# Four-layer transformer kernel: router in column groups, picks ahead of the extra turns, token parts by halves, modulation chunks of layer 0 moved

## Chip, cores, metric

One core of one Trainium2 chip. The time is the device time of one execution in microseconds. The kernel before takes 2621.84 us, the median of three runs (2620.9 to 2629.41).

## What is computed

x has 256 tokens of 1024 values, in float32. Two blocks of two layers each are applied. In the kernel's count, layers 0 and 1 are the first block (attention and a gated feed-forward part with a short convolution), layers 2 and 3 the second (a state-space and a gated linear-attention mixer, then a feed-forward part). Each layer is modulated by a vector that is computed from c by a 1024 x 6144 product. Layer 3's feed-forward part is a mixture of eight experts; the change is mostly about it:

```python
def _moe_swiglu(x, w_router, b_router, w_gate, w_up, w_down):
    logits = (x @ w_router).astype(jnp.float32) + b_router.astype(jnp.float32)
    top_vals, top_idx = lax.top_k(logits, TOP_K)            # TOP_K = 2
    top_w = jax.nn.softmax(top_vals, axis=-1)
    combine = jnp.sum(jax.nn.one_hot(top_idx, N_EXPERTS, dtype=jnp.float32) * top_w[..., None], axis=-2)
    out = jnp.zeros_like(x)
    for e in range(N_EXPERTS):                              # N_EXPERTS = 8, width 3584
        out = out + combine[..., e:e + 1].astype(x.dtype) * _swiglu(x, w_gate[e], w_up[e], w_down[e])
    return out
```

## The kernel before

It is written by hand for five engines, each with its own instruction list; semaphores order them, and every wait stands in the code. Weights come in chunks of 1 MB through a ring of seven slots; SyncE issues the loads in the order of chunk_plan, each as soon as TensorE has used the chunk seven places before. ScalarE (ACT) writes a chunk's leading part in fp32r, VectorE (DVE) or GpSimd (POOL) the rest in place, and TensorE (PE) sums three products of such parts (lines 847 to 849), which gives float32 exactness at the fp32r rate.

**Layer 0, projections (PE lines 1226 on, DVE line 2765).** Fifteen column chunks in the order PROJ_ORDER. The first three (i = 0, 1, 2) are multiplied whole in float32 (L675), the others by parts. The parts of hT are written by ACT early and by DVE (L2769), on DVE behind the low part (L2106) of the fourth chunk. After each projection one of layer 0's modulation chunks 8 to 23 is multiplied (ada_sum, L577: eight products of 256 columns in four column groups of the array), two after the last.

**Normalization of layers 2 and 3 (post_layer, DVE L2246 to L2264).** For each half t of the tokens: gate, residual, statistics, a power on POOL (L1393), centring (L2264, "normed"). PE transposes x (L615), ACT and DVE evict the blocks of hT with scale and shift (blocks b = 0, 2 by ACT, 1, 3 by DVE), and POOL meanwhile applies gain and shift to x itself (gains, L1417 and L1419, four operations on 128x1024).

**Router (PE L1259, L1261; DVE route, L2701).** For each half of the tokens eight products of hT's 128 columns (as weights) with the router's 8 columns, then the bias. DVE copies the logits (L2705), takes the maximum, the differences (L2709, which ACT exponentiates), ranks every logit against the others, and marks the two best ("chosen").

**Places, picks, extra turns (DVE mixture, L2306).** An expert has room for 128 tokens; an expert chosen by more gets an extra turn, up to three. PE counts places with five small products (L1182 to L1185); DVE makes the places (L2315 on; "placed"), then the list of turns with the extra ones (L2327 to L2346; "turns"), then the selection matrices pick and pick_w of the first turn (picks, L2350, L2351). xn, in which the output is summed, is set to zero at L2311. PE gathers the first expert's tokens (pick_tiles, L1118), ACT writes them with scale and shift as xg in eight pieces and then its leading part xg_hi whole, DVE the low part whole (x_part, L2361).

**Expert turns (body).** A turn has 42 chunks: for g = 0 to 6 two of gate and two of up, then, one group later, two of down. The first turn ("first") is written out, the others are a loop over turns. PE waits for moe_lo (DVE, L2371) or, for every second down chunk, moe_lo_pool (POOL, L1361). Near the end of a turn (j = 37) PE gathers the next expert's tokens. At the turn's last step ACT writes xg and xg_hi and then the leading part of the transposed products; DVE writes their low part (L2386) and xg's. In the profile w_gate is loaded 126 times, 14 for each of nine turns.

## Time and profile before

| | us |
|---|---|
| median of three runs | 2621.84 |
| the profiled execution | 2623.3 |
| its span, first to last instruction | 2621.5 |
| mean granted TensorE clock | 0.974 of full |
| PE busy | 2487.1 (95%) |
| DVE busy | 1792.8 (68%) |
| ACT busy | 1320.4 (50%) |
| POOL busy | 675.3 (26%) |
| HBM read | 691.10 MB, 264 GB/s over the span |

A row of a timeline gives start, duration, engine, line, operation, output and inputs, the count of merged instructions, and in brackets the idle time in front of it with what ended it. A float32 product shows as two instructions. "ring" and "region" are the weight slots and the working space, with the ending _part when they are written as fp32r. L1468 is the helper of all ACT operations.

### The profile page before, as it was taken

What the parts mean: (1) busy time and instruction counts of PE and PEld (TensorE: products, weight loads), DVE (VectorE), ACT (ScalarE), POOL (GpSimd) and SP (SyncE); (2) the same over time, 40 slices, a digit from 0 to 9 for tenths busy, and PEclk for the clock granted to TensorE, in tenths of its full rate; (3) what the DMA queues carried; (4) which work ended last, traced back from release to release, by engine and by line L of the source; (5) the groups of instructions that cost most, each with busy time, mean ns of one, the idle gap of its engine ahead of it and who ended that gap; (6) DMA issues with size and microseconds to landing.
All of it is one profiled execution on the core that took longest, in us unless ns stands there. A gap on an engine that the chain in (4) does not pass through costs nothing. (4 is left out here: it accounts for less than half of the span.)

```text
span 2621.5 us, 37532 instructions
## 1 busy us (share of the span) xinstructions
PE 2487.1 (95%) x14758; PEld 2043.2 (78%) x14758; DVE 1792.8 (68%) x2022; ACT 1320.4 (50%) x1368; POOL 675.3 (26%) x355
## 2 busy tenths in 40 slices
PE   6999999998999998999887999999999999999996
PEld 4875998985998767899674787878787888888884
DVE  1664776574866947755874777777778777777785
ACT  1434543444443133333131676767676766677773
POOL 0000000003900808700631132323232332323223
PEclk9999999999999998999997999999999999999998
DMA  9996864476874756955332899999999999999992
GB/s 338 288 322 219 260 204 149 154 258 218 263 217 147 237 197 218 288 185 167 107 113 66 303 347 349 348 351 346 346 350 345 344 351 338 357 334 361 327 366 109
DMA packets 434956, 693.86 MB, mean 265 GB/s; under 512 B 37690, under 2 KB 255894, under 8 KB 434838
## 3 DMA queue, kind: packets, MB, share of 16 engines
q1 hardware_dynamic: 407632, 677.17, 75.2%
q10 hardware_dynamic: 27206, 15.03, 2.1%
q8 instruction: 85, 1.39, 0.2%
q14 instruction: 33, 0.27, 0.0%
HBM read 691.10 MB, written 1.05 MB: 264 GB/s over the span
## 5 line engine op out<-in xcount | busy, mean ns | idle before, releaser
L1468 ACT ACTIVATE region_part<-ring 128x2048 fp32r<-128x2048 f32 x448 | 835.6, 1907 | 274.0 <-PE bank L849 194.6
L849 PE MATMUL bank<-ring_part,region_part 128*128 128x512 f32 x1648 | 648.7, 394 | 0.0
L2371 DVE TENSOR_TENSOR ring_part<-ring,region_part 128x2048 fp32r<-128x2048 f32 x270 | 640.4, 2405 | 1.7 <-ACT region_part L1468 1.7
L847 PE MATMUL bank<-region_part 128*128 128x512 f32 x1432 | 582.3, 407 | 6.2 <-DVE ring_part L2371 6.2
L848 PE MATMUL bank<-region_part 128*128 128x512 f32 x1296 | 511.7, 395 | 0.0
L1361 POOL TENSOR_TENSOR ring_part<-ring,region_part 128x2048 fp32r<-128x2048 f32 x54 | 268.2, 4974 | 554.8 <-ACT region_part L1468 554.8
L849 PEld LDWEIGHTS bank<-ring_part,region_part 128*128 128x128 f32 x1648 | 309.7, 188 | 71.3
L847 PE MATMUL bank<-xn_part,region_part 128*128 128x256 f32 x1152 | 327.3, 284 | 10.0 <-DVE hT_part L2074 9.1
L847 PEld LDWEIGHTS bank<-region_part 128*128 128x128 f32 x1432 | 269.4, 188 | 75.5 <-issue 14.6
L849 PE MATMUL bank<-hT_part,region_part 128*128 128x256 f32 x1152 | 325.6, 283 | 0.0
L848 PE MATMUL bank<-xn_part,ring_part 128*128 128x256 f32 x1152 | 325.4, 282 | 0.0
L2029 DVE TENSOR_TENSOR ring_part<-ring,region_part 128x2048 fp32r<-128x2048 f32 x72 | 175.4, 2444 | 177.5 <-ACT region_part L1468 177.5
L1393 POOL TENSOR_TENSOR stat<-stat,minus_half 128x1 f32<-128x1 f32 (+1 forms) x36 | 21.7, 602 | 1058.0 <-DVE stat L2005 580.7
L848 PEld LDWEIGHTS bank<-region_part 128*128 128x128 f32 x1296 | 243.6, 188 | 60.1 <-issue 7.7
L1468 ACT ACTIVATE region<-bank 128x512 f32<-128x512 f32 (+1 forms) x172 | 94.5, 573 | 366.2 <-PE bank L849 241.1
L847 PEld LDWEIGHTS bank<-xn_part,region_part 128*128 128x128 f32 x1152 | 219.3, 190 | 14.7 <-DVE hT_part L2074 10.7
L848 PEld LDWEIGHTS bank<-xn_part,ring_part 128*128 128x128 f32 x1152 | 220.1, 191 | 1.4
L849 PEld LDWEIGHTS bank<-hT_part,region_part 128*128 128x128 f32 x1152 | 219.4, 190 | 0.0
L2382 DVE TENSOR_TENSOR region<-bank,region 128x512 f32<-128x512 f32 x63 | 43.5, 691 | 167.7 <-issue 166.8
L1361 POOL TENSOR_TENSOR ring_part<-ring,hT_part 128x2048 fp32r<-128x2048 f32 x9 | 55.5, 6172 | 286.6 <-ACT hT_part L1468 286.6
L1468 ACT ACTIVATE region_part<-bank 128x512 fp32r<-128x512 f32 x63 | 37.6, 597 | 165.2 <-PE bank L1161 165.2
L577 PE MATMUL bank<-ring,c_wide 128*32 128x256 f32 x1536 | 105.0, 401 | 9.3 <-DMA ring<-in_w_ada 9.3
(321 smaller groups left out, 3990.4 us busy)
## 6 DMA issues: line engine op xcount, KB each, us to landing
ring<-in_moe_w_gate SPq DMA_DIRECT2D x126, 1024.0 KB, 5.1
ring<-in_moe_w_up SPq DMA_DIRECT2D x126, 1024.0 KB, 5.2
ring<-in_moe_w_down SPq DMA_DIRECT2D x126, 1024.0 KB, 5.0
ring<-in_w_ada SPq DMA_DIRECT2D x48, 1024.0 KB, 7.4
ring<-in_mod_w SPq DMA_DIRECT2D x48, 1024.0 KB, 6.7
ring<-in_w_in SPq DMA_DIRECT2D x44, 1024.0 KB, 5.7
ring<-in_w_up_act SPq DMA_DIRECT2D x22, 1024.0 KB, 5.5
ring<-in_w_up_lin SPq DMA_DIRECT2D x22, 1024.0 KB, 5.8
```

The costliest lines, as they stand in the source:

```text
L577: m = nc.tensor.matmul(o[r:r + 32, 0:CW], c_wide[:, k, AT - q:AT - q + 32], w[:, k, :], start=q == first and k < 4, stop=k >= 4, skip_grou ...
L847: nc.tensor.matmul(o, split(a_hi), split(b_hi), start=start, stop=False, skip_group_check=True)
L848: nc.tensor.matmul(o, split(a_lo), split(b_hi), start=False, stop=False, skip_group_check=True)
L849: return nc.tensor.matmul(o, split(a_hi), split(b_lo), start=False, stop=stop, skip_group_check=True)
L1361: nc.gpsimd.tensor_tensor(split(w), w, whole(hi), ALU.subtract).then_inc(*done("moe_lo_pool", j, e))
L1393: nc.gpsimd.tensor_tensor(dst, dst, minus_half[:, 0:dst.shape[1]], ALU.pow).then_inc(*done("rstd", *key))
L1468: return nc.scalar.activation(out_, in_, func, **kw).then_inc(*done(*event))
L2029: v.tensor_tensor(split(chunk(key)), chunk(key), whole(hi_part(key)), ALU.subtract).then_inc(*done("w_lo", *key))
L2371: v.tensor_tensor(split(w), w, whole(hi), ALU.subtract).then_inc(*done("moe_lo", j, e))
L2382: v.tensor_tensor(moe_h, psum[2 * (g % 2) + 1], moe_s, ALU.mult).then_inc(*done("moe_h", g, e))
```

## The change

Layer 0's modulation chunks: none after the first three projections, then one or two after each. The router multiplies hT (256 columns) by 8-column weights in four column groups, two blocks k in each, as the blocks become ready; the bias is added third; ACT and DVE copy the four groups' partial sums into router_out (the place of spread, set to zero before), two more products turn them, and DVE's reduction adds the four groups. POOL's gains wait for both halves of the normalization. xn is set to zero by POOL behind the gains. The extra turns are computed behind the first turn's picks, low parts and token parts, with the first three low parts brought forward. Both picks come before both pick_w, and the gather waits only for the picks. xg_hi and xg's low part are made in two halves, and TensorE waits for the second half only at the second chunk.

```diff
@@ -62,6 +62,8 @@
 IN_WHOLE = 3
+ADA_FIRST = {3: (8,), 4: (9,), 5: (10,), 6: (11,), 7: (12,), 8: (13,), 9: (14, 15), 10: (16,), 11: (17, 18), 12: (19,), 13: (20, 21),
+             14: (22, 23)}
 IDX_PAIRS = [((0, 0), (0, 1)), ((1, 0), (1, 1)), ((1, 2), (1, 3))]
@@ -235,7 +237,7 @@
                 if l == 0:
-                    for q in ([8 + i] if i < 14 else [22, 23]):
+                    for q in ADA_FIRST.get(i, ()):
                         plan.append((("ada", 0, q), ("pe_used", "ada", 0, q)))
@@ -430,6 +432,7 @@
     moe_hi = [cm("", n=SLOT) for _ in range(SLOTS - 1)] + [hT.rearrange("p k s -> p (k s)")]
+    router_out = spread
     turns = nc.alloc_sbuf_tensor("turns", [P, TURNS], mybir.dt.int32)[:, :]
@@ -1102,6 +1105,33 @@
+            def route():
+                halves = [bank(("router", h), ("logits", h), (5 + h,)) for h in range(2)]
+                logits = bank(("logits",), ("logits", 2), (7,))
+                pe.wait_ge(*until("router_loaded"))
+                pe.wait_ge(*until("router_b_loaded"))
+                for b in range(4):
+                    pe.wait_ge(*until("hTd" if b % 2 else "hT", 3, "ffn", b))
+                    for i in range(2):
+                        k = 2 * b + i
+                        g = k % 4
+                        m = nc.tensor.matmul(halves[g // 2][32 * g:32 * g + NE, 0:S], router[:, k, :], hT[:, k, :],
+                                             start=k < 4, stop=k >= 4, skip_group_check=True)
+                    if b == 1:
+                        for t in range(NT):
+                            nc.tensor.matmul(halves[0][0:NE, t * P:(t + 1) * P], router_b[0:1, :], ones[0:1, :],
+                                             start=False, stop=False, skip_group_check=True)
+                    if b >= 2:
+                        m.then_inc(*done("pe_tile", "router", b - 2))
+                pe.wait_ge(*until("router_out", 1))
+                pe.wait_ge(*until("logits", 1))
+                pieces = ident.rearrange("p (g c) -> p g c", g=4)[:, :, 0:NE]
+                for t in range(NT):
+                    m = nc.tensor.matmul(logits[:, t * 4 * NE:(t + 1) * 4 * NE].rearrange("p (g c) -> p g c", g=4),
+                                         router_out[:, t * P:(t + 1) * P], pieces, start=True, stop=True)
+                m.then_inc(*done("pe_tile", "logits"))
             def mixture():
@@ -1110,7 +1140,7 @@
                         pe.wait_ge(*until("x_gained", 3, "mix", 1))
-                    pe.wait_ge(*(until("moe_pick", e) if r is None else within(r, 0, "moe_pick", e)))
+                    pe.wait_ge(*(until("moe_pick_one", 1, e) if r is None else within(r, 0, "moe_pick_one", 1, e)))
                     for b in range(2):
@@ -1128,8 +1158,8 @@
                     for j, (what, g, a) in enumerate(TURN):
-                        if j == 0:
-                            pe.wait_ge(*(until("moe_xg_lo", "start") if r is None else within(r, 1, "moe_xg_lo", e)))
+                        if j < 2:
+                            pe.wait_ge(*(until("moe_xg_lo", j, "start") if r is None else within(r, 1, "moe_xg_lo", j, e)))
                         if what == "gate" and a == 0:
@@ -1229,7 +1259,7 @@
                         if l == 0:
-                            for q in ([8 + i] if i < 14 else [22, 23]):
+                            for q in ADA_FIRST.get(i, ()):
                                 ada_sum(0, 1, q, 8)
@@ -1250,17 +1280,7 @@
                 if l == 3:
-                    hT_ready(l, "ffn")
-                    pe.wait_ge(*until("router_loaded"))
-                    pe.wait_ge(*until("router_b_loaded"))
-                    o = bank(("router",), ("logits",))
-                    for t in range(NT):
-                        for k in range(KD):
-                            nc.tensor.matmul(o[:, t * NE:(t + 1) * NE], hT[:, k, t * P:(t + 1) * P], router[:, k, :],
-                                             start=k == 0, stop=False)
-                        m = nc.tensor.matmul(o[:, t * NE:(t + 1) * NE], ones[0:1, :], router_b[0:1, :],
-                                             start=False, stop=True)
-                    m.then_inc(*done("pe_tile", "router"))
+                    route()
                     mixture()
@@ -1412,6 +1432,7 @@
                 pool.wait_ge(*until(f"rows_{stage}{l}", 1))
+                pool.wait_ge(*until("normed", l, stage, 1))
                 for t in range(NT):
@@ -1452,6 +1473,7 @@
                     gains(l, "mix")
+                    nc.gpsimd.memset(xn, 0.0).then_inc(*done("x_gained", l, "mix", 2))
                     mixture()
@@ -1755,8 +1777,8 @@
                                 scale=scale_col[:, 1, k:k + 1], bias=mod_col[:, 1, 24 + k:25 + k])
-                    act.wait_ge(*(until("moe_xg", KD - 1, e) if r is None else within(r, 0, "moe_xg", KD - 1, e)))
-                    run(split(xg_hi), xg, ACT.Copy, "moe_xg_hi", e)
+                        act.wait_ge(*(until("moe_xg", 4 * b + 3, e) if r is None else within(r, 0, "moe_xg", 4 * b + 3, e)))
+                        run(split(xg_hi[:, 4 * b:4 * b + 4, :]), xg[:, 4 * b:4 * b + 4, :], ACT.Copy, "moe_xg_hi", b, e)
@@ -1790,7 +1812,7 @@
-                act.wait_ge(*until("pe_tile", "router"))
+                act.wait_ge(*until("pe_tile", "router", 1))
                 for j in range(3):
@@ -1931,6 +1953,9 @@
                     load(iota, A["const_iota"], "const_moe", 1)
+                    p_ = tile("router", 0)
+                    for g in range(2):
+                        run(router_out[32 * g:32 * g + NE, :], p_[32 * g:32 * g + NE, 0:S], ACT.Copy, "router_out", g)
                     act.wait_ge(*until("moe_shift"))
@@ -2308,7 +2333,6 @@
                 v.memset(weight, 0.0).then_inc(*link())
-                v.memset(xn, 0.0).then_inc(*link())
                 p_ = tile("places")
@@ -2317,15 +2341,22 @@
                 after()
-                v.tensor_scalar(place[:, :, 0:NE], place[:, :, 0:NE], -1.0, None, ALU.add).then_inc(*link())
-                v.tensor_tensor_scan(rank, ones[:, 0:1].broadcast_to([P, NE]), over, 0.0, ALU.mult, ALU.add).then_inc(*link())
+                v.tensor_scalar(place[:, :, 0:NE], place[:, :, 0:NE], -1.0, None, ALU.add).then_inc(*done("placed"))
                 v.tensor_copy(weight[:, :, 0:NE], cb).then_inc(*link())
+                dve.wait_ge(*until("const_moe", 1))
                 after()
-                v.memset(stat[:, 60:61], 0.0).then_inc(*done("placed"))
-                dve.wait_ge(*until("const_moe", 1))
-                v.tensor_copy(turns[:, 1:NE], iota[:, 1:NE]).then_inc(*link())
-                for j in range(EXTRA):
+                def extra_turns():
+                    v.tensor_tensor_scan(rank, ones[:, 0:1].broadcast_to([P, NE]), over, 0.0, ALU.mult, ALU.add).then_inc(*link())
+                    v.tensor_copy(turns[:, 1:NE], iota[:, 1:NE]).then_inc(*link())
+                    for j in range(EXTRA):
+                        extra_turn(j)
+                    after()
+                    v.tensor_scalar(place[:, :, NE:TURNS], place[:, :, NE:TURNS], float(-CAP), None, ALU.add).then_inc(*link())
+                    after()
+                    v.tensor_scalar(turns[:, 0:1], rank[:, NE - 1:NE], NE - 1.0, None, ALU.add).then_inc(*done("turns"))
+                def extra_turn(j):
                     is_jth = hot[:, 0, :]
@@ -2340,16 +2371,13 @@
                         v.tensor_reduce(what[:, :, NE + j], mine, AX.X, ALU.add).then_inc(*link())
-                after()
-                v.tensor_scalar(place[:, :, NE:TURNS], place[:, :, NE:TURNS], float(-CAP), None, ALU.add).then_inc(*link())
-                after()
-                v.tensor_scalar(turns[:, 0:1], rank[:, NE - 1:NE], NE - 1.0, None, ALU.add).then_inc(*done("turns"))
...
                     for t in range(NT):
-                        v.tensor_scalar(pick[:, t, :], iota, place[:, t, at], None, ALU.is_equal).then_inc(*done("moe_pick_one", 2 * t, e))
+                        v.tensor_scalar(pick[:, t, :], iota, place[:, t, at], None, ALU.is_equal).then_inc(*done("moe_pick_one", t, e))
+                    for t in range(NT):
                         v.tensor_scalar(pick_w[:, t, :], iota, place[:, t, at], weight[:, t, at], ALU.is_equal, ALU.mult)\
-                            .then_inc(*(done("moe_pick", e) if t else done("moe_pick_one", 1, e)))
+                            .then_inc(*(done("moe_pick", e) if t else done("moe_pick_one", 2, e)))
@@ -2357,18 +2385,23 @@
                 def x_part(e, r):
-                    dve.wait_ge(*(until("moe_xg_hi", e) if r is None else within(r, 0, "moe_xg_hi", e)))
-                    v.tensor_tensor(split(xg), xg, whole(xg_hi), ALU.subtract).then_inc(*done("moe_xg_lo", e))
+                    for b in range(2):
+                        ks = slice(4 * b, 4 * b + 4)
+                        dve.wait_ge(*(until("moe_xg_hi", b, e) if r is None else within(r, 0, "moe_xg_hi", b, e)))
+                        v.tensor_tensor(split(xg[:, ks, :]), xg[:, ks, :], whole(xg_hi[:, ks, :]), ALU.subtract).then_inc(*done("moe_xg_lo", b, e))
+                def low_part(j, e, now):
+                    dve.wait_ge(*now("moe_hi", j))
+                    hi, w = moe_parts(e, j)
+                    v.tensor_tensor(split(w), w, whole(hi), ALU.subtract).then_inc(*done("moe_lo", j, e))
...
                     for j in range(CHUNKS):
-                        if not by_pool(j):
-                            dve.wait_ge(*now("moe_hi", j))
-                            hi, w = moe_parts(e, j)
-                            v.tensor_tensor(split(w), w, whole(hi), ALU.subtract).then_inc(*done("moe_lo", j, e))
+                        if not by_pool(j) and (r is not None or j > 2):
+                            low_part(j, e, now)
                         if j - 2 in Z_AT and r is not None:
@@ -2391,7 +2424,11 @@
                 picks("start", slice(0, 1))
+                for j in range(3):
+                    low_part(j, "first", lambda *ev: until(*ev, "first"))
                 x_part("start", None)
+                extra_turns()
+                dve.wait_ge(*until("x_gained", 3, "mix", 2))
                 body("first", None)
@@ -2701,8 +2738,12 @@
                 lg, m1, sh, ex, cb = moe[:, 0], moe[:, 1], moe[:, 6], moe[:, 7], moe[:, 9]
-                p_ = tile("router")
-                v.tensor_copy(lg, p_[:, 0:NT * NE].rearrange("p (t e) -> p t e", t=NT)).then_inc(*done("logits"))
+                p_ = tile("router", 1)
+                for g in (2, 3):
+                    v.tensor_copy(router_out[32 * g:32 * g + NE, :], p_[32 * g:32 * g + NE, 0:S]).then_inc(*done("logits", g - 2))
+                p_ = tile("logits")
+                v.tensor_reduce(lg, p_[:, 0:NT * 4 * NE].rearrange("p (t g e) -> p t e g", t=NT, g=4), AX.X, ALU.add)\
+                    .then_inc(*done("logits", 2))
                 after()
@@ -2819,6 +2860,7 @@
                 else:
+                    v.memset(router_out, 0.0).then_inc(*link())
                     norm(l, "ffn")
```

## Rows read from the trace of the kernel before

**Rows 1.** windows: us, busy PE PEld DVE ACT POOL, PEclk, DMA share, GB/s
```profile
1443.70:1446.00 2.30, 0.00 (x0) 0.00 (x0) 0.00 (x0) 2.27 (x5) 0.00 (x0) 1.00 0.00 0
...
2000.00:2500.00 500.00, 500.00 (x2263) 403.72 (x2262) 381.04 (x230) 351.69 (x269) 140.85 (x28) 1.00 0.97 347
```

**Rows 2.** timeline, DVE, layer normalization of layers 2 and 3: start us, us
```profile
1258.50 2.82 DVE L2264 TENSOR_SCALAR x<-x,stat 128x1024 f32<-128x1024 f32 x1 [0.67 <-POOL stat L1393]
...
1402.54 0.81 DVE L2264 TENSOR_SCALAR x<-x,stat 128x1024 f32<-128x1024 f32 x1 [0.66 <-POOL stat L1393]
...
1409.34 2.82 DVE L2264 TENSOR_SCALAR x<-x,stat 128x1024 f32<-128x1024 f32 x1 [0.67 <-POOL stat L1393]
```

**Rows 3.** timeline, POOL, gain and shift in front of the router
```profile
1409.27 2.34 POOL L1417 TENSOR_TENSOR x<-x,rows 128x1024 f32<-128x1024 f32 x1
...
1416.75 2.35 POOL L1419 TENSOR_TENSOR x<-x,rows 128x1024 f32<-128x1024 f32 x1
```

**Rows 4.** timeline, DVE and POOL at the start of layer 3
```profile
1266.42 2.84 DVE L2551 TENSOR_TENSOR region<-region,s5p 128x512 f32<-128x512 f32 x1
...
1275.07 0.69 DVE L2595 TENSOR_TENSOR region<-region,bank 128x512 f32<-128x512 f32 x1 [3.03 <-PE bank L959]
...
1268.66 0.95 POOL L1439 MEMSET ffn_rows<- 128x1024 f32 x1
```

**Rows 5.** timeline, PE, modulation chunk, router, places, picks
```profile
22.72 1.93 PE L577 MATMUL bank<-ring,c_wide 128*32 128x256 f32 x16 [1.39 <-DMA ring<-in_w_ada]
...
1415.37 3.55 PE L1259 MATMUL bank<-router,hT 128*128 128x8 f32 x16 [1.19 <-ACT hT L1468]
...
1426.65 0.60 PE L1182 MATMUL bank<-moe,region 128*128 128x8 f32 x2 [3.18 <-DVE moe L2724]
...
1428.38 0.57 PE L1185 MATMUL bank<-moe,ones 128*128 128x8 f32 x2
...
1436.92 6.70 PE L1118 MATMUL bank<-region,x 128*128 128x128 f32 x32 [7.97 <-DVE region L2351]
```

**Rows 6.** timeline, DVE, from the router to the picks
```profile
1423.51 0.17 DVE L2705 COPY moe<-bank 128x16 f32<-128x16 f32 x1 [8.24 <-PE bank L1261]
...
1423.93 0.17 DVE L2709 TENSOR_TENSOR moe<-moe 128x16 f32<-128x16 f32 x1
...
1427.94 1.76 DVE L2311 MEMSET xn<- 128x2048 f32 x1 [0.38 <-issue]
...
1429.81 0.17 DVE L2315 SCALAR_TENSOR_TENSOR region<-bank,moe 128x16 f32<-128x16 f32 x1
...
1435.72 0.15 DVE L2346 TENSOR_SCALAR turns<-moe 128x1 int32<-128x1 f32 x1
```

**Rows 7.** timeline, ACT, DVE and PE, first token parts and chunks
```profile
1440.71 1.50 ACT L1468 ACTIVATE region<-bank,mod_col,scale_col 128x128 f32<-128x128 f32 x4 [10.96 <-PE bank L1118]
...
1446.29 1.22 DVE L2361 TENSOR_TENSOR region_part<-region,region_part 128x1024 fp32r<-128x1024 f32 x1 [9.51 <-ACT region_part L1468]
...
1447.43 4.49 DVE L2371 TENSOR_TENSOR ring_part<-ring,region_part 128x2048 fp32r<-128x2048 f32 x2
...
1449.86 0.77 PE L847 MATMUL bank<-region_part 128*128 128x512 f32 x1 [6.23 <-DVE ring_part L2371]
...
1459.84 0.39 PE L847 MATMUL bank<-region_part 128*128 128x512 f32 x1
```

**Rows 8.** timeline, PE, DVE and SP queue, projections of layer 0
```profile
56.96 3.79 PE L675 MATMUL bank<-ring,hT 128*128 128x72 f32 x32
...
65.70 0.55 PE L847 MATMUL bank<-region_part,xn_part 128*128 128x256 f32 x1 [3.94 <-DVE hT_part L2769]
...
62.85 2.49 DVE L2769 TENSOR_TENSOR hT_part<-hT,xn_part 128x512 fp32r<-128x512 f32 x4
...
133.42 49.93 SPq L1280 DMA_DIRECT2D ring<-in_w_ada  x16
```

**Rows 9.** timeline, DVE, end of an expert's turn
```profile
1694.56 0.69 DVE L2386 TENSOR_TENSOR region_part<-bank,region_part 128x512 fp32r<-128x512 f32 x1 [3.76 <-ACT region_part L1468]
```

## Prediction, made before the kernel was run

> **What bounds the kernel now.** I read the windows by stage first. From 2000 to 2500 us TensorE is busy 500.00 of 500 us at full granted clock [rows 1], and it is so from about 1460 to 2585 us: nine turns of the expert body (eight experts and one extra turn), each the same matmuls. No edit here takes a matmul out of a turn, so the loop's length stands and whatever makes its first chunks start earlier is kept to the end. The DMA engines are 0.97 busy there [rows 1], close behind, but it is TensorE that has no gap.
>
> Then I read the timeline of each engine over the only long stretch in which TensorE idles, 1405 to 1450 us: layer 3's normalization, the router, the places, the picks, the token parts. It is one chain through PE, DVE, ACT and POOL, and TensorE runs at its lower clock in it. There every microsecond is on the path. The other edited place is layer 0's first projections, where a load bounds one step.
>
> **Gains after the normalization (POOL).** DVE's centring takes 0.81 us alone and 2.82 us in the two cases where POOL's multiplication by the gain has begun 0.07 us before it [rows 2, 3]: POOL started at 1409.27 and DVE, issued at 1409.34, came through only when POOL was done. The new wait puts POOL behind DVE. Before the router this makes x ready 2.01 us earlier, and the same at the end of layer 2. Behind the new wait on POOL stand its four gain operations, then xn's memset, then nothing until the experts' ninth chunk. In layer 2's mixer DVE already wins; nothing there.
>
> Start of layer 3: the transposes start 2.0 us earlier, the gains end about 1 us later, so DVE's two-input operations there (L2550 on) wait for the port longer. One such operation took 2.84 us instead of 0.69 [rows 4]: it was held until POOL's last gain operation ended at 1268.66. With four POOL operations from 1259.35 on, I place the end of that DVE group at about 1272.8 (now 1272.04: DVE idles 3.03 before 1275.07); the first S5 unit's tiles come at 1275.07 - 2.0 = 1273.07 [rows 4]. It just fits, so **2.0 us** are kept (bounds 0.5 and 2.0).
>
> **Router.** The old form starts at 1415.37 and its sum reaches DVE at 1423.51 [rows 5, 6]: 8.14 us. The new form sends 256 columns through 8-column weights in four column groups. The nearest row is a layer-0 modulation chunk, the same eight 256-column products in four groups: 1.93 us at the lower clock [rows 5], so a quarter of the serial time. Six of the eight run as their blocks of hT arrive; the last pair takes 0.85, and the two bias products (0.43 each, group 0) push it by up to 0.4. From the last block: 1.4 us of PE, two copies on each of ACT and DVE 0.95, four short PE instructions 1.0, three hand-overs 0.1 each: DVE reduces 3.8 us after the old router's start. In the old frame that is 1419.2 against 1423.51, **4.3 us** (bounds 2.5, if the groups serialize, and 5.5). The zeroing of router_out by DVE lies in its wait for the transposes.
>
> But this and the 2.0 us run into POOL. Its gains took 1409.27 to 1419.10 [rows 3]; behind the new wait, without the 0.3 us that they lost to DVE, they run 1410.2 to 1419.75. DVE's reduced logits would be there at 1417.25 and the first operation with two SBUF inputs (L2709, 1423.93 now [rows 6]) at 1417.7. As the L2551 row shows [rows 4], such an operation waits for the POOL operation under way: until 1419.75. So the chain moves by 1423.93 - 1419.75 = **4.2 us**, not 6.2. POOL's memset of xn comes next and doesn't hold it: L2551 ran its 0.6 us inside POOL's MEMSET [rows 4]. Bounds: 6.2 if small operations slip through, 3.5 if more than one waits.
>
> The Trainium skill's page "SBUF — State Buffer", section "Who interferes with whom", states the same split: a VectorE instruction with two SBUF inputs contends with a GpSimd instruction that reads SBUF and not with one that only writes. It speaks against this change in so far as the router is brought forward into POOL's gains; without it the sum would be 2.0 us larger.
>
> **Places to picks.** Five products on PE, 1426.65 to 1428.95, stay [rows 5]. DVE then is still in its memset of xn (1427.94 to 1429.70) and starts at 1429.81 [rows 6]; with the memset on POOL it starts at 1429.03: 0.8 us. Then 7.11 us go by until the pick products start at 1436.92 [rows 5, 6], most of them the extra turns' chain of small operations, which ends at 1435.87 [rows 6]. What stays in front of the picks is three small steps and two operations of 0.28: 1.15 us. **0.8 + 5.96 = 6.8 us** (bounds 6.0 and 7.0). The pick products themselves now start at P = 1436.92 - 4.2 - 6.8 = 1426.0; x's last gain (1419.75) is ready.
>
> **Token parts by halves, low parts first.** All from P, the start of the pick products; they take 6.70 [rows 5]. Now the first expert product starts at P + 12.94 (1449.86) and the fourth chunk at P + 22.92 (1459.84) [rows 7]. After: ACT takes the first half at P + 3.8 (1440.71 now), 1.5 us, then its leading part 0.6, ready at P + 6.1. DVE after the picks does three low parts, 2.25 each (two in 4.49 [rows 7]), P + 0.3 to P + 7.0, and only then the half token part, 0.62 (half of 1.22 [rows 7]). TensorE starts at P + 7.75, 1.05 us behind the picks. Now, the clock has reached full level as the picks end (1.00 over 1443.70 to 1446.00 [rows 1]) and is lost before 1449.86; after, it should be kept.
>
> What is late next is DVE: the second half's part ends at P + 9.6, and there stand the extra turns, 5.6 us (1435.87 less 1429.81 and the 0.45 of three steps that are not theirs [rows 6]), to P + 15.2, and then the fourth chunk's low part, 2.25: P + 17.6. TensorE at full clock would want it at P + 7.75 + 36 x 0.233 = P + 16.1, so it waits 1.5 us. Behind the extra turns on DVE stand that low part and all later ones, and PE waits for them. The fourth chunk starts at P + 17.65 against P + 22.92: **5.3 us**. After that DVE needs 2.25 us a chunk and TensorE 2.8, so the lead grows again; ring, ACT and POOL are ahead. Bounds 4.0 (DVE short again at chunks 5 to 8) and 6.8 (the extra turns run faster). The first ring load after the start now shares the DMA engines with the rows load of ACT, 1 MB; its chunk is wanted four chunks later, so this is free.
>
> Expert stage: 4.2 + 6.8 + 5.3 = **16.3 us**. In the loop the halves cost ACT and DVE about 0.1 us each at a turn's end, under cover of TensorE.
>
> **Layer 0.** TensorE ends the third projection at 60.7, does a modulation chunk and idles 3.94 us until 65.70, waiting for hT's low part (DVE 62.85 to 65.3), which stood behind the fourth chunk's low part, whose load came late [rows 8]. Without the three modulation chunks (1.01 each) the third projection ends at 58.7, its weights and the fourth chunk being three loads nearer to the front; DVE starts hT's part at once, 2.49 us, and TensorE goes on at 61.4. That is 4.3 us, but the three chunks come back later in a stretch where TensorE is busy: 3.0. **1.3 us** is kept. In the last six slots ten modulation chunks share the queue with six of the projection: 16 MB at 3.1 us each (16 in 49.93 [rows 8]) against 45 us of TensorE, 5 us short, which the seven slots ahead cover: the last weight lands about 4 us before it is wanted. Bounds: -3 if they don't cover, +3.5 if the shorter wait keeps the clock at full (the spell at half clock after 65.70 costs 2.2 us).
>
> **Sum.** 2.0 + 16.3 + 1.3 = 19.6 us. The profiled execution is 2623.3 us, so 2603.7; it is 1.5 us over the median of the runs, 2621.84, which gives 2602.2. I predict 2602.5.
>
> **The rivals.**
> (A) The sum, 2600 to 2606: chance 0.55.
> (B) The port doesn't hold the router's small operations, or layer 0 keeps its clock: 2621.84 - 21.5 or more, 2597 to 2600. For it: no row shows an operation as small as 16 elements held. Against it: the rows of larger ones. Chance 0.17. That the port holds it is also the Trainium skill's rule named above.
> (C) Terms fall short: DVE has no lead behind the extra turns and TensorE waits in chunks 5 to 8 (1.5 us each at most), column groups serialize (1.8), layer 0 gives nothing (1.3), layer 3 loses its 2.0. Two or three of them: 2606 to 2613. Chance 0.22. For it: three of the hidden places have under 1 us to spare.
> (D) The change doesn't do what it says: the routing chain is shorter, but TensorE then waits for weights in the first turn until it is where it was. Seven slots are full before 1410 and later ones land in 5 us; within 0.3%, 2614 to 2622: chance 0.03.
> (E) Slower: the turns get longer. At a turn's end ACT writes the token part in two pieces with a wait between, in front of the transposed part on which DVE's L2386 waits (1694.56 to 1695.25 [rows 9]); TensorE wants it at 1696.50, 1.25 us later. If ACT came 1.25 us late TensorE would wait in each of eight turns; from 1.25 + 19.6/8 = 3.7 us late on the kernel is slower, and at 5 us it takes 2632. ACT idles 0.6 us in front of it and the split costs it 0.1. Chance 0.03.
>
> Only about 0.3% (8 us) can be told from no change here. Faster by more: A, B, C: 0.94; within: 0.03; slower: 0.03. The range holds A, most of B and two thirds of C: 2597.5 to 2610.
>
> **What would show it.** DVE's L2264 at 0.81 in all six cases. POOL's gains from 0.05 us after it. L2709 starting as POOL's last gain ends, not when the reduce is done. PE's picks 10.9 us earlier against the same landmark. One gap of about 1 us before the first expert product, one of 1.5 us before the fourth chunk, full clock in between. In layer 0 a gap of 2.7 us instead of 3.9. Turns of the same length. The prediction is wrong if a turn's length changes, if TensorE waits for DVE's low parts after the fourth chunk, or if loads hold up the end of layer 0's projections.

## The result, and the profile after

| | before | after |
|---|---|---|
| median of the runs side by side | 2624.47 us | 2602.47 us |
| runs, from and to | 2620.9 to 2629.41 | 2598.74 to 2604.59 |
| profiled execution | 2623.3 us | 2600.72 us |
| its span | 2621.5 us | 2598.9 us |
| mean granted TensorE clock | 0.974 | 0.978 |

The ratio is 0.9909, with a 95% interval of 0.9891 to 0.9928: 22 us faster. In the profiled executions the difference is 22.6 us, and it falls into two parts. Up to the start of the last centring on DVE (1409.34 before [rows 2], 1404.05 after) 5.3 us are gained; from there to the start of the second turn's picks 17.3 us; behind that nothing, since every later turn takes 127.01 us in both. Of the executions behind this document one of the changed kernel, in the run a_again, took 3022.14 us at a mean granted clock of 0.774, and no comparison uses it.

The stage in front of the router, after. This is VectorE's timeline from the last centring to the picks (start, duration, engine, line, operation, in brackets the idle time before it and what ended it); some rows between are left out:

```profile
1404.05 0.81 DVE L2289 TENSOR_SCALAR x<-x,stat 128x1024 f32<-128x1024 f32 x1 [0.67 <-POOL stat L1413]
...
1412.25 0.23 DVE L2745 TENSOR_REDUCE moe<-bank 128x16 f32<-128x64 f32 x1 [1.22 <-PE bank L1131]
1412.51 0.17 DVE L2748 TENSOR_REDUCE moe<-moe 128x2 f32<-128x16 f32 x1
1412.72 1.81 DVE L2750 TENSOR_TENSOR moe<-moe 128x16 f32<-128x16 f32 x1
1414.45 0.21 DVE L2755 TENSOR_TENSOR moe_pair<-moe 128x64 f32<-128x64 f32 x1
...
1419.42 0.17 DVE L2339 SCALAR_TENSOR_TENSOR region<-bank,moe 128x16 f32<-128x16 f32 x1 [1.43 <-PE bank L1215]
...
1420.06 0.48 DVE L2377 TENSOR_SCALAR region<-region 128x128 f32<-128x128 f32 x2
```

And GpSimd's, with the last of its four gain operations and the memset that it took over:

```profile
1404.99 2.36 POOL L1438 TENSOR_TENSOR x<-x,rows 128x1024 f32<-128x1024 f32 x1 [0.98 <-issue]
...
1412.16 2.34 POOL L1440 TENSOR_TENSOR x<-x,rows 128x1024 f32<-128x1024 f32 x1
1414.44 1.80 POOL L1476 MEMSET xn<- 128x2048 f32 x1
```

Read the two together. The centring takes 0.81 us, since GpSimd starts behind it (2.82 in [rows 2]). The row to learn from is L2750, the comparison that is L2709 in the kernel before: an operation of 16 elements a partition that took 0.17 us before [rows 6] lasts 1.81 us, until GpSimd's last gain operation ends at 1414.50. The two reductions just ahead of it are not held, and the next ones run at 0.21 us inside GpSimd's MEMSET.

TensorE's timeline, from the new router to the fourth chunk of the first expert turn:

```profile
1406.87 1.28 PE L1119 MATMUL bank<-hT,router 128*8 128x256 f32 x8
1408.08 1.01 PE L1123 MATMUL bank<-ones,router_b 1*8 1x128 f32 x4
1409.02 1.04 PE L1119 MATMUL bank<-hT,router 128*8 128x256 f32 x8
1411.18 1.03 PE L1131 MATMUL bank<-ident_sb,region 128*128 128x32 f32 x4 [1.12 <-DVE region L2743]
...
1420.69 5.59 PE L1148 MATMUL bank<-region,x 128*128 128x128 f32 x32 [1.31 <-DVE region L2377]
1428.32 0.50 PE L850 MATMUL bank<-region_part 128*128 128x512 f32 x1 [2.03 <-DVE region_part L2391]
...
1437.12 0.50 PE L850 MATMUL bank<-region_part 128*128 128x512 f32 x1 [0.18 <-DVE ring_part L2396]
```

The router's products end at 1410.06, and the logits reach VectorE's reduction 8.20 us behind the start of the centring; before they came 14.17 us behind it [rows 2, 6]. The picks' products start 16.64 us behind the start of the centring (27.58 before [rows 2, 5]). The first expert product comes 7.63 us behind the picks (12.94 before [rows 5, 7]), the fourth chunk 16.43 (22.92). From 1428.32 to 1437.00 the granted clock is 1.00, and the products, but for the first of a stretch, take 0.39 us and start 0.23 us apart: the clock is kept.

Layer 0, first TensorE's row, where the fourth projection starts; then two rows of DVE, the making of hT's low part, which now does not stand behind the fourth chunk's weights, and the last copy of layer 0's modulation:

```profile
60.24 0.55 PE L850 MATMUL bank<-region_part,xn_part 128*128 128x256 f32 x1 [2.90 <-DVE hT_part L2810]
```
```profile
57.38 2.50 DVE L2810 TENSOR_TENSOR hT_part<-hT,xn_part 128x512 fp32r<-128x512 f32 x4 [5.71 <-PE bank L678]
...
153.27 0.42 DVE L1998 COPY mod_acc<-bank 128x256 f32<-128x256 f32 x1 [5.04 <-PE bank L580]
```

Before, those were 65.70 with 3.94 us of idle time [rows 8], and the copy came at 155.99.

### The profile page after: what moved, and what is told of

It reads as the page before. It is cut to its first block and busy times, and to the rows that moved or that the text cites. A ratio compares the mean times of both kernels' runs of the same rounds, so it can differ in the third digit from the quotient of the medians.

```text
span 2598.9 us, 37561 instructions
## 1 busy us (share of the span) xinstructions
PE 2481.1 (95%) x14746; PEld 2035.9 (78%) x14746; DVE 1793.5 (69%) x2033; ACT 1322.2 (51%) x1380; POOL 676.7 (26%) x356
## 5 line engine op out<-in xcount | busy, mean ns | idle before, releaser
L851 PE MATMUL bank<-region_part,ffn_rows_part 128*128 128x512 f32 x288 | 113.2, 393 | 0.0
```

The costliest lines, as they stand in the source:

```text
L851: nc.tensor.matmul(o, split(a_lo), split(b_hi), start=False, stop=False, skip_group_check=True)
```

## Experiments

One execution of one and the same kernel differs from the next by several microseconds, so parts worth 0.5 to 5 us can't be told from medians of four runs alone. They can be told from distances inside a stage: these repeat to 0.1 us where the clock is the same. The changed kernel run a second time (a_again) shows how well.

> The changed kernel once more, as the reference on the same chip for the runs beside it. Every theory expects 2602.5 us (2599 to 2605), 0.991 of the kernel before, and the stage's own distances again: from the start of the last centring to the first gather 16.6 us, from there to the first expert product 7.6 us and to the fourth chunk's product 16.4 us.

Measured: median 2604.16 us of the three executions that are compared (2605.43 with the fourth), ratio 0.9923 (0.9899 to 0.9947). The distances were 16.63, 7.62 and 16.43 us, against 16.64, 7.63 and 16.43. In the table C is the start of the last centring, P the start of the first picks' products (TensorE's gather of the first expert's tokens), P2 that of the second turn's; all in us.

| kernel | centring | P - C | first product - P | fourth chunk - P | P2 - C |
|---|---|---|---|---|---|
| before | 2.82 | 27.58 | 12.94 | 22.92 | 150.59 |
| after | 0.81 | 16.64 | 7.63 | 16.43 | 133.30 |
| a_again | 0.81 | 16.63 | 7.62 | 16.43 | 133.23 |
| e_nowait | 2.82 | 15.99 | 7.62 | 16.42 | 132.63 |
| e_waitonce | 2.82 | 17.02 | 7.63 | 16.34 | 133.55 |
| e_oldrouter | 0.81 | 18.91 | 7.63 | 16.80 | 135.94 |
| e_both | 2.82 | 20.92 | 7.63 | 17.24 | 138.39 |
| e_defer | 0.81 | 15.00 | 7.63 | 16.85 | 137.36 |
| e_memset | 0.81 | 17.45 | 7.62 | 16.10 | 133.73 |
| e_turnsfirst | 0.81 | 22.03 | 7.63 | 16.09 | 138.23 |
| e_whole | 0.81 | 16.63 | 9.60 | 19.61 | 136.31 |
| e_lowlater | 0.81 | 16.63 | 11.09 | 23.04 | 141.44 |

**The wait on GpSimd, and the floor.** The theory of the prediction: the router's chain can't be earlier than GpSimd's last gain, whatever is saved ahead of it. The rival: each part is worth what it saves by itself.

```diff
 e_nowait
-                pool.wait_ge(*until("normed", l, stage, 1))
```

> The changed kernel, but GpSimd does not wait for the second token half to be centred before its first gain; the whole result is computed. Theory (GpSimd's last gain is the floor of the router's chain, because VectorE's first operation with two SBUF inputs runs only when it ends): the centring lasts 2.8 us instead of 0.8 at two places; layer 3 starts 2.0 us later, but in the router's stage GpSimd starts and so ends its gains some 0.6 us earlier in proportion to the centring, the logits are there 2.0 us later, and the first gather moves by less than 1 us. Total +1.9 to +2.9 us on the changed kernel. Rival (no floor: the wait is worth its 2.0 us at both places): +4.0 us, and the gather 18.6 us behind the centring's start.

Measured: 2605.25 us, ratio 0.9921 (0.9902 to 0.994). The centring is 2.82 us long again at both places. From layer 2's last statistics to layer 3's first the four kernels in which GpSimd doesn't wait (before, e_nowait, e_ada, e_both) show 144.03 to 144.45 us, all others 142.11 to 142.95: the wait is worth 1.7 us there on the means. Before the router the gather came not later, as both theory and rival had it, but 0.65 us earlier. The clock rose in the middle of the router in this run, as these rows of TensorE show:

```profile
1416.18 0.81 PE L1123 MATMUL bank<-ones,router_b 1*8 1x128 f32 x4
1416.92 0.62 PE L1119 MATMUL bank<-hT,router 128*8 128x256 f32 x8
```

The faster products brought the logits 9.16 us behind C, and VectorE's first comparison, 0.21 us long, ended at C + 9.84, beside GpSimd's last gain at C + 9.80. To tell the clock from the wait, the wait was taken away at the router alone:

```diff
 e_waitonce
-                pool.wait_ge(*until("normed", l, stage, 1))
+                if l != 3:
+                    pool.wait_ge(*until("normed", l, stage, 1))
```

> The changed kernel, but GpSimd waits for the centring only ahead of layer 3, not ahead of the last router; the whole result is computed. If the wait is worth its 2.0 us at the first place and costs 0.65 us at the second (GpSimd's gains are then the last thing ready), this is the best of both: gather at 16.0 us behind the centring's start, layer 3's first centring at 142.1 to 143.0 us behind layer 2's last statistics, total 0.65 us shorter than the changed kernel, which is less than one comparison of medians can tell. Rival (the 0.65 us came from the clock, which was back at its full level early in that run by chance): gather at 16.8 us.

Measured: 2602.37 us, ratio 0.9909 (0.9892 to 0.9925); P - C is 17.02, with the router at the lower clock as in the changed kernel. So the rival of that run holds, near 16.8: without the risen clock the gather isn't earlier. But the clock could give the 0.65 us only because the wait was gone: with it GpSimd's last gain ends at C + 10.45, without it at C + 9.78 to 9.80, so the wait moves the floor itself 0.65 us later. Here the logits come at C + 10.22, behind the floor. The wait saves 2.01 us of centring at this place and 0.38 us of the chain. It is no better kernel: its median is that of the changed one.

```diff
 e_oldrouter (route() as before; no copies, no turning products, no memset of router_out)
...
-                    for i in range(2):
-                        k = 2 * b + i
-                        g = k % 4
-                        m = nc.tensor.matmul(halves[g // 2][32 * g:32 * g + NE, 0:S], router[:, k, :], hT[:, k, :],
...
+                    for k in range(KD):
+                        nc.tensor.matmul(o[:, t * NE:(t + 1) * NE], hT[:, k, t * P:(t + 1) * P], router[:, k, :],
...
```

> The changed kernel with the router's products as in the kernel before: one row group, 32 products of four columns groups' worth in a row, bias last, no turning products; the whole result is computed. By themselves these products take 4.3 us more than the grouped ones. Theory (the port floor): the first gather moves by the time by which the old router's end lies behind GpSimd's last gain only, some 2 us: centring's start to gather 18.8 us, total +2.2 us. Rival (no floor, the grouping is worth all it saves by itself): 20.9 us and +4.3 us.

Measured: 2607.0 us, ratio 0.9927 (0.9907 to 0.9947), P - C 18.91: +2.27, as the theory had it, against 4.3 by the rival. Then both were undone together:

```diff
 e_both
 e_oldrouter, and
-                pool.wait_ge(*until("normed", l, stage, 1))
```

> The changed kernel with two parts undone together: the router's products as in the kernel before, and GpSimd not waiting for the centring; the whole result is computed. Undone alone, the first moved the gather from 16.64 to 18.91 us behind the centring's start, the second to 15.99. Theory (the later of two ends counts: the router's products, or GpSimd's last gain): with both undone the products end last by far, and the gather stands at 20.6 to 20.9 us, as in the kernel before less the 0.8 us of the memset and the 5.9 us of the extra turns. Rival (each part has a cost of its own, and they add): 2.27 - 0.65 = 1.6 us over the changed kernel, 18.3 us. Layer 3's first centring 144.0 to 144.5 us behind layer 2's last statistics instead of 142.1 to 143.0.

Measured: 2609.45 us, ratio 0.9944 (0.9924 to 0.9964), P - C 20.92. Undone alone the two cost 2.27 and 0.38 us, together 4.28. They don't add: in the changed kernel the later end is GpSimd's, so the first microseconds that either part loses cost nothing. That slack is 1.63 us: L2750 ends at C + 10.48, and without gains beside it (e_defer, below) the same operation ends at C + 8.85. By themselves the two parts delay the end of the comparison by 3.91 and 2.02 us; less 1.63 each gives 2.28 and 0.39, and both together, 5.92, less 1.63 give 4.29. In e_both the later end is the products': the copy of the logits comes at 1420.43, when GpSimd's last gain has been over since 1416.02.

```profile
1413.67 2.35 POOL L1426 TENSOR_TENSOR x<-x,rows 128x1024 f32<-128x1024 f32 x1
```
```profile
1420.43 0.17 DVE L2725 COPY moe<-bank 128x16 f32<-128x16 f32 x1 [8.25 <-PE bank L1118]
...
1420.84 0.18 DVE L2729 TENSOR_TENSOR moe<-moe 128x16 f32<-128x16 f32 x1
```

**Taking the floor away.** If GpSimd's gains hold the router, they can go elsewhere.

```diff
 e_defer (GpSimd: the gains one by one behind its first four low parts of the first turn)
-                    gains(l, "mix")
+                    pool.wait_ge(*until("normed", l, "mix", 1))
...
+                            if r is None:
+                                gain_step(j)
...
-                                scale=scale_col[:, 1, k:k + 1], bias=mod_col[:, 1, 24 + k:25 + k])
+                                scale=fused[:, 0, k:k + 1] if e == "start" else scale_col[:, 1, k:k + 1],
+                                bias=fused[:, 1, k:k + 1] if e == "start" else mod_col[:, 1, 24 + k:25 + k])
```

> The changed kernel, but GpSimd's four gain operations on x before the last expert stage are put between its low-part operations of the first turn, and the gathered rows of the first turn take the gain on ScalarE from the fused scale and shift; the whole result is computed. Theory (port floor): VectorE's first comparison in the router lasts 0.2 us instead of 1.8, the picks come 1.5 to 2.0 us earlier (centring's start to first gather 14.6 to 15.1 us), and the total falls by up to 2.0 us to about 2600.5, if the gains do not delay the first turn's low parts. Rival (the comparison is long by itself, or the gains, now beside VectorE's two-input operations, cost in the turn what they cost before it): the comparison still lasts 1.8 us, or the fourth chunk's product comes as late as in the changed kernel; total +0 to +3 us.

Three things more differ in this run: the clearing of xn stands where the gains stood, the first picks don't wait for the gains, and ScalarE issues its loads of rows behind the first turn instead of ahead of it.

Measured: 2607.44 us, ratio 0.9929 (0.991 to 0.9947). In front of the picks the theory holds: the comparison lasts 0.18 us, the gather is 1.64 us earlier. The total goes the rival's way: the first turn is 122.36 us long instead of 116.66, and 4.1 us are lost at P2. Here are a gain of GpSimd and VectorE's low parts in that turn, then two low parts at the same place in the changed kernel:

```profile
1418.84 0.18 DVE L2769 TENSOR_TENSOR moe<-moe 128x16 f32<-128x16 f32 x1
...
1457.59 8.13 DVE L2415 TENSOR_TENSOR ring_part<-ring,region_part 128x2048 fp32r<-128x2048 f32 x2
```
```profile
1459.13 4.45 POOL L1387 TENSOR_TENSOR x<-x,rows 128x1024 f32<-128x1024 f32 x1
```
```profile
1452.68 5.93 DVE L2396 TENSOR_TENSOR ring_part<-ring,region_part 128x2048 fp32r<-128x2048 f32 x2
```

Three of the four gains take 4.44 to 4.45 us instead of 2.34 (the other 2.41), and the two low parts 8.13 instead of 5.93: each pays for the other. TensorE feels it. In the changed kernel it has no gap over 0.1 us between the fourth chunk and P2; here it has six that the profile puts down to a low part of VectorE or GpSimd, of 0.27 to 1.76 us, and each also costs about 0.1 us at the restart. The place in front of the router was the cheap one for these four operations: there they cost 1.64 us.

**The memset of xn, and the extra turns.**

```diff
 e_memset
-                    nc.gpsimd.memset(xn, 0.0).then_inc(*done("x_gained", l, "mix", 2))
+                v.memset(xn, 0.0).then_inc(*link())
...
```

> The changed kernel with the clearing of xn back on VectorE between the weights and the places, as before; the whole result is computed. Theory (on the path, at its price on VectorE): the gather at 17.4 us behind the centring's start instead of 16.64, +0.8 us in the total. Rival (VectorE waits there anyway for the places' matmuls, which start from the chosen experts and not from the memset): the gather stays at 16.6 us.

Measured: 2604.2 us (two runs), ratio 0.9916 (0.9895 to 0.9937), P - C 17.45: +0.81 us. The operation is 1.76 us long; the rest of it hid in the wait for the places' products.

```diff
 e_turnsfirst
+                extra_turns()
                 picks("start", slice(0, 1))
                 for j in range(3):
                     low_part(j, "first", lambda *ev: until(*ev, "first"))
                 x_part("start", None)
-                extra_turns()
```

> The changed kernel with VectorE's count of the extra turns put back between the places and the picks; the whole result is computed. Theory (it runs on the path to the first gather): its 5.5 us come back in full there, centring's start to gather 22.1 us instead of 16.6; behind the gather the first product stays at 7.6 us and the fourth chunk's at 16.1 to 16.4, so the total is 5.2 to 5.5 us longer. Rival (behind the gather the count costs as much as ahead of it, because it holds up VectorE's low parts): the gather is 5.5 us later but the fourth chunk comes 3 us or more earlier behind it, so that less than 2.5 us are lost.

Measured: 2607.7 us, ratio 0.9941 (0.992 to 0.9961), P - C 22.03: +5.39 us. Behind P the fourth chunk came 0.34 us earlier and P2 - C is 4.93 us longer. So nearly the whole count of the extra turns was on the path in front of the picks, and next to nothing of it is behind them.

**Halves and low parts.**

```diff
 e_whole
-                        run(split(xg_hi[:, 4 * b:4 * b + 4, :]), xg[:, 4 * b:4 * b + 4, :], ACT.Copy, "moe_xg_hi", b, e)
+                    run(split(xg_hi), xg, ACT.Copy, "moe_xg_hi", e)
...
```

> The changed kernel with the token parts of the first expert pass taken whole again instead of in two halves (one copy of 128x1024 on ScalarE, one subtraction on VectorE, and the first product waits for both); the whole result is computed. Theory (the first product is what the halves bring forward, and the fourth chunk follows it without a stall): the first product comes 1.7 to 3.2 us later behind the gather's start, at 9.3 to 10.8 us instead of 7.6, and the fourth chunk's as much later than 16.4. Rival (the low parts of the fourth chunk set the pace, the halves are hidden): the first product is later but the fourth chunk stays at 16.4 us. Gather at 16.6 us behind the centring's start in both.

The edit takes the halves out of every turn, not of the first alone; the other turns keep their 127.01 us.

Measured: 2607.78 us, ratio 0.9941 (0.9922 to 0.9961). The first product comes 1.97 us later, P2 3.0 us. Part of the difference is the clock. TensorE idles 3.94 us, starts at full speed (granted clock 1.00 from 1432.10 to 1433.20), and falls to its lower level (0.50 from 1433.20 to 1436.40); rows of this run, from the first products and from where it ends:

```profile
1432.10 0.50 PE L850 MATMUL bank<-region_part 128*128 128x512 f32 x1 [3.94 <-DVE region_part L2389]
...
1433.48 0.63 PE L852 MATMUL bank<-ring_part,region_part 128*128 128x512 f32 x1
...
1436.04 0.63 PE L852 MATMUL bank<-ring_part,region_part 128*128 128x512 f32 x1
1436.46 0.46 PE L850 MATMUL bank<-region_part 128*128 128x512 f32 x1
1436.76 0.39 PE L851 MATMUL bank<-region_part 128*128 128x512 f32 x1
```

Products at 0.63 us start 0.43 us apart instead of 0.23; some eight of them make 1.6 us, of which the missing stalls behind them take part back. After idle times of 0.99 to 2.39 us at this place (ten runs) the clock stayed full.

```diff
 e_lowlater
-                for j in range(3):
-                    low_part(j, "first", lambda *ev: until(*ev, "first"))
                 x_part("start", None)
+                for j in range(3):
+                    low_part(j, "first", lambda *ev: until(*ev, "first"))
                 extra_turns()
```

> The changed kernel with VectorE's first three low parts of weights put back behind the tokens' low parts; the whole result is computed. Theory (VectorE has nothing else to do while the gather runs, so the three low parts of 2.2 us each are free there and nowhere else): the third product of the first chunk waits for its low part until 10.8 to 11.2 us behind the gather's start, and the fourth chunk's product comes at 21.7 to 23.1 us instead of 16.43. Rival (PE is the bound by then and VectorE catches up, as the extra turns can wait): the fourth chunk at 18 us or earlier.

Measured: 2610.89 us (two runs), ratio 0.9942 (0.992 to 0.9963); first product at 11.09, where the expectation had only the third wait so long; fourth chunk at 23.04, P2 8.1 us later. This is the largest single item: 6.6 us up to the fourth chunk, and 1.5 us behind it, where some eight products run at or near 0.63 us, at the clock's lower level, after TensorE has idled 2.02 us. Idle times as long left the clock full in other runs, so the length of one gap alone doesn't tell. VectorE's timeline behind the picks shows where the first part comes from, 5.62 us of waiting for ScalarE that the low parts filled in the changed kernel:

```profile
1419.89 0.60 DVE L2379 TENSOR_SCALAR region<-region 128x128 f32<-128x128 f32 x2
1426.12 0.69 DVE L2391 TENSOR_TENSOR region_part<-region,region_part 128x512 fp32r<-128x512 f32 x1 [5.62 <-ACT region_part L1490]
1428.17 0.69 DVE L2391 TENSOR_TENSOR region_part<-region,region_part 128x512 fp32r<-128x512 f32 x1 [1.37 <-ACT region_part L1490]
1428.78 4.49 DVE L2396 TENSOR_TENSOR ring_part<-ring,region_part 128x2048 fp32r<-128x2048 f32 x2
```

**Layer 0's table.**

```diff
 e_ada: before, with
-                    for q in ([8 + i] if i < 14 else [22, 23]):
+                    for q in ADA_FIRST.get(i, ()):
 e_noada: after, with the reverse
```

> The kernel before with one part of the change alone: the modulation chunks between the projections of layer 0 start at the fourth slot (the table ADA_FIRST). The router, the picks and the token parts are as before; the whole result is computed. Theory A (the prediction's sum): the fourth projection starts 4.3 us earlier but the clock falls earlier too, and 1.3 us are left: layer 0's last modulation copy at 154.7 us instead of 155.99. Theory B (what the changed kernel's profile showed): 2.7 us are left, the copy at 153.3. Total: 2622.0 us by A, 2620.6 by B, beside 2623.3 profiled; the stages from the last centring on are as in the kernel before, with 27.6 us from there to the first gather.

> The changed kernel without the new table: one modulation chunk after every projection slot from the first on, as in the kernel before; the whole result is computed. Theory A: layer 0 is 1.3 us longer, the last modulation copy at 154.6 us instead of 153.27. Theory B: 2.7 us, at 156.0. If the two parts do not act on each other, this is the mirror of the run that adds the table to the kernel before. The stage of the last router stays as in the changed kernel: 16.6 us from the centring to the first gather.

Measured: e_ada against before 0.9993 (0.9981 to 1.0005), which tells nothing; e_noada 2606.66 us, 0.9934 (0.9916 to 0.9953). The landmarks tell more. With the table (twelve kernels) the fourth projection starts at 59.84 to 61.48 us, always after 2.90 us of idle time, and the last copy comes at 152.67 to 153.81. Without it (before and e_noada) they are 65.70 and 65.66, and 155.99 and 154.93. Here TensorE waits for hT's low part, which VectorE makes behind the fourth chunk's low part; ScalarE's share of that chunk, at 58.65, had waited 11.24 us for its load (e_noada, for comparison with the row of the changed kernel above):

```profile
65.66 0.55 PE L850 MATMUL bank<-region_part,xn_part 128*128 128x256 f32 x1 [5.06 <-DVE hT_part L2810]
```

The means of the copy are 153.0 and 155.5: 2.5 us, nearer to theory B, though e_noada alone shows 1.9. The clock differs between the two without the table: behind this gap the products run at the lower level (granted 0.50) for 2.9 us in e_noada and for 5.2 us in before.

## Why the prediction was right, point by point

**Expert stage: 17.3 us against 16.3.** The steps up to the picks came as worked out. The logits came 5.97 us earlier, of which 2.01 are the centring's, so the router by itself gave 3.96 us for 4.3. But the comparison ended only 4.28 us earlier (10.48 us behind the centring's start, 14.76 before) for a predicted 4.2, and e_oldrouter, e_both and e_defer show that GpSimd's gains set it. The memset gave 0.82 (5.71 us from the end of the comparison to L2339's counterpart before [rows 6], 4.89 after), which e_memset repeats with 0.81. The extra turns gave 5.84: 7.11 us were left behind the places, 1.27 are. Together 10.94, predicted 10.9. The rule of the Trainium skill, "SBUF — State Buffer", section "Who interferes with whom", is borne out by the held L2750 and by the reductions and the run inside MEMSET that were not held; e_defer shows the operation at 0.18 us once no GpSimd operation reads beside it.

The term that was mis-sized is the one behind the picks, 6.35 us at P2 (123.01 against 116.66) for a predicted 5.3. The first product was right, 7.63 for 7.75. The stall before the fourth chunk was 0.18 us for 1.5: the second half's part ended at P + 8.74, not P + 9.6, and the extra turns took 5.4 us, not 5.6, so the fourth chunk's low part began at P + 14.08 instead of P + 15.2. The clock rose earlier, so that the picks' 32 products took 5.59 us instead of 6.70 [rows 5]. This changed nothing here: the first product stands at 7.6 us in ten runs with products of 5.24 to 6.63 us.

**Layer 3's start: 2.0 us.** Kept nearly: 1.9 us between before and after, 1.7 on the means of all runs. What the prediction feared, VectorE's group held longer by GpSimd, took place within the slack: the first unit's tile came at 1269.60, 5.47 us earlier than [rows 4], as the transposes of x started 5.40 us earlier, and in front of the tile DVE idled 0.61 us instead of 3.03.

**Layer 0: 2.7 us between the profiles (2.5 on means) against 1.3.** The mechanism was right: the projections run through, the wait for hT's low part stays (2.90 us; foreseen 2.7), the clock falls again, and the three chunks come back later: of 5.46 us at the start of the fourth projection 2.72 are left at the copy. The term that was too small is the start of the fourth projection, put at 61.4. It was 60.24 in the profiled run and 60.6 on the mean of the twelve, because the third projection ended at 57.34 and not at 58.7. No load held up the end of the projections: ScalarE waited for weights up to 8.45 us in the profile after, but TensorE shows no idle time over 0.15 us from 60.24 to 155 us.

**The turns** have the same length, 127.01 us: the split of the token parts cost nothing, and the slower case fell away.

**The sum** was 19.6 us, and 22.6 came in the profiled executions: 1.0 more behind the router, 1.4 more in layer 0, and 0.6 in stretches that the change doesn't touch (2.3 gained ahead of layer 2's first statistics, 1.6 lost in layer 2); that spells of the clock made them is likely and not shown. The medians are 22.0 apart, but the median before was 2624.47 beside this one and 2621.84 in the runs on which the prediction was made; so the time itself, 2602.47 us, fell so close to the predicted 2602.5 by luck. The mechanisms were confirmed one by one, the total to within 3 us.

What each part is worth at P2, undone alone: router 2.6 us (with the wait 5.1), memset 0.4, extra turns 4.9, halves 3.0, low parts 8.1. This makes 21.6 us (with router and wait as one) for a stage that gained 17.3, so the parts of a chain are not to be added: halves and low parts both shorten the same wait of TensorE.

## What to carry to other kernels

On a serial chain across engines, list for each step the ends that it waits for, and look for the second-latest before pricing an edit: the router's grouping brought the logits 4.0 us forward and was worth 2.3, because GpSimd's last gain came next. Where a neighbour's work costs least has to be measured: here GpSimd's four gains cost 1.64 us in front of the router and 5.7 us in the first turn, where both engines are busy with low parts. Compare parts of a microsecond by distances inside a stage, not by totals, and note the clock at both ends.

## What the runs showed of the hardware beyond that

- A VectorE operation of 16 elements a partition with two SBUF inputs was held by GpSimd's operation on 1024 elements until that ended: 1.80 to 1.84 us instead of 0.17, in all seven runs in which the two met in this way. Its small size did not help it through.
- The race that the new wait ends is still there once, at the end of the changed kernel. The first row is GpSimd's, the second VectorE's:

```profile
2590.40 2.34 POOL L1424 TENSOR_TENSOR x<-xn,rows 128x1024 f32<-128x1024 f32 x1
```
```profile
2590.47 2.82 DVE L2320 TENSOR_SCALAR xn<-x,stat 128x1024 f32<-128x1024 f32 x1 [0.67 <-POOL stat L1413]
```

  No run shows what a wait would be worth there.
- The clock adds a few microseconds that belong to no edit. VectorE has the first statistics of layer 2 together (its BATCH_NORM_AGGREGATE) between 981.5 and 986.9 us in the twelve kernels with the same program up to there. At the very end, from the start of the last turn's picks to that of VectorE's last addition, eleven of the fourteen kernels take 41.2 us and three 43.6 to 44.0. The same two products of TensorE show the difference, first in the changed kernel, then in e_nowait:

```profile
2573.67 1.12 PE L1155 MATMUL bank<-region 128*128 128x512 f32 x2 [0.78 <-DVE xn L2385]
```
```profile
2580.03 2.07 PE L1155 MATMUL bank<-region 128*128 128x512 f32 x2 [0.79 <-DVE xn L2384]
```

  They take 1.12 us where the granted clock is 0.97 of the 2.4 GHz (2573.40 to 2578.40) and 2.07 us where it is 0.50, that is 1.2 GHz (2578.80 to 2583.80). Three such pairs make the 2.8 us by which e_nowait's end is longer. Why one execution loses the clock there and another does not stays open.
